# Two attention stages of one encoder layer change places, and their filler products are dealt out anew

## The chip, the cores and the metric

The kernel runs on one core of one Trainium2 chip, in one launch. The metric is the device time of a run in microseconds (us); it was 2349.54 us, the median of three runs (2349.14 to 2350.11). All arrays are fp32. Products on TensorE (PE) are made accurate by splitting each operand into a rounded high part and a low rest and doing three passes (low by high, high by high, high by low). The other engines are VectorE (DVE), ScalarE (ACT), GpSimd (POOL); SyncE (SP) issues nearly all DMAs.

## The reference, cut to what matters

One layer is computed for two request groups with shared weights: a prompt of 1024 positions, and a sample of 64 new positions that follow 2048 cached ones.

```python
h    = rms_norm(x, g_pre_mix)
u_a, v_a, q, k, v_b = split(h @ w_in)                      # 5 blocks of 1024 columns
y_a  = gelu(u_a) * (tril(w_s[g]) @ layer_norm(gelu(v_a)) + b_s)
# stick-breaking attention: 16 heads of 64, strictly causal, no softmax
z    = q @ k.T / 8;  A = sigmoid(z) * prod over later keys of sigmoid(-z);  y_b = A @ v
g_a, g_b = split(sigmoid(h @ w_gate + b_gate))             # 2 x 1024 columns
m    = g_a * (y_a @ w_branch_a) + g_b * (y_b @ w_branch_b)
x    = x + rms_norm(m @ w_o, g_post_mix)
x    = x + rms_norm(conv_ffn(rms_norm(x, g_pre_ffn)), g_post_ffn)
```

For the sample group, `k` and `v_b` are appended to the cache (`cache_sb_k`, `cache_sb_v`), so its attention runs over 2112 keys. The gates need only `h`, branch A only `y_a` and its half of the gates: neither depends on an attention.

## The kernel before, in words

Prompt and sample positions lie side by side in one axis of 1092 columns (2 gap columns, 1024, 2 more, 64), cut into three chunks of 364. A *fill* is one matmul of 128 x 128 weights by one chunk; 24 fills (8 tiles of the inner dimension by 3 passes) make a *group*, and 3 groups a *block* of 128 output columns (72 fills). `feature_part` (line 246) issues them. The weights of a block pass through `Weights` (line 109): SP loads 512 KB into one of two raw buffers, POOL splits them into a high and a low slot (`split_one`, lines 145 to 151), PE waits in `ready`. Two such slots rotate in both attention stages.

The stages run one after the other. Each is an `nc.Block` with an instruction stream of its own for every engine, written out by hand: each engine works through its stream in order, with waits on semaphores. At the end of a stage (`Sems.give_back`, line 86) all engines meet in a barrier, after SP has waited for the last stores.

1. `phase_project`: `h` is made and turned (`hT`, high and low, region r0); 40 blocks of `h @ w_in`; q, k, v, y_a go to DRAM scratch. PE ends with nine transposes (line 467) and POOL with a last low part, then SP stores v.
2. `phase_prompt_attention` (line 668): 16 heads of 4 *windows*; a window is a couple of 128-query tiles (0-1, 2-3, 4-5, 6-7, in the order `TURNS`). The windows are cut into 96 *units*. In a unit PE transposes weights (`turn`), scores the window two further on (`score`, `LEAD` = 2), multiplies fills between the scores, and adds up the unit before (`weighted_sum`). ACT makes two sigmoids of each score (lines 942, 943) and the high parts (952), DVE the running product (`scan`, 990) and the low parts (998), POOL the product of both (`weigh`, 818). The fills are all 16 gate blocks, 1152 of them, 10 to 16 in a unit (`DENSE`), 72 in a head; ACT puts the sigmoid on each group and SP stores it.
3. `phase_sample_attention` (line 1019): 8 pairs of heads in *steps* t = -1 to 8. In step t PE follows `PLAN`: scores z0 to z4 of pair t, transposes A0 to A4 of pair t-1's weights, transposes K0 to K3 of pair t+1's cached keys, and at the end `weighted_sum` of pair t-1. DVE's order in a step is A2, `scan_high`, A3, a gated product, A4, `scan_low`, `weigh_low`, K0 to K3; POOL does `split_v`, `weigh_high`, `split_w`. The transposes go through three PSUM buffers, so item n waits for the low part of item n-3. The fills are the 8 blocks of branch A (576), 72 in each of the steps 1 to 8 (`PIECES`). They need `yaT`, which takes the place of `hT`: in steps -1 and 0 there are no fills, and y_a is loaded in 8 pieces of 546 KB through two stage buffers (`load_ya`), rounded by ACT (`ya_hi`, line 1322) and completed by DVE (`ya_lo`, 1374). DVE multiplies each group by its gate (`gated`, 1380), loaded from scratch, and the product `ta` is stored.
4. `phase_merge`: loads `yb`, multiplies branch B, adds `ta`. Then `phase_output` and `phase_ffn`.

## Time and profile before

| | value |
|---|---|
| median of three runs | 2349.54 us (2349.14 to 2350.11) |
| the profiled execution's own time | 2349.76 us |
| its span (first to last instruction) | 2347.8 us |
| mean granted clock of TensorE | 0.963 of full |
| busy: PE, PE weight load, DVE, ACT, POOL | 92%, 88%, 56%, 32%, 37% of the span |
| project stage, last PE instruction | ends at about 559.5 us |
| prompt attention, PE | 579.5 to 1007.8 us |
| sample attention, PE | 1017.9 to 1252.0 us |
| merge, first matmul | 1273.6 us |

The busy time of an engine is the sum of its instructions' spans; a matmul's span includes its way through the array, so that at full clock fills start every 0.17 us though each is shown with 0.33 us. A PE busy time equal to the length of a stretch means that PE had no gap, not that its array was full. The granted clock is a share of the full one: 1.00 and 0.50 are the two levels (2.4 and 1.2 GHz).

### The profile page before, as it was taken

How to read it: one execution, taken by the hardware profiler on the slowest of the kernel's cores; microseconds unless marked ns; L12 is line 12 of the kernel's file. 1: busy time of each engine (PE TensorE's matmuls, PEld its weight loads, DVE VectorE, ACT ScalarE, POOL GpSimd, SP SyncE). 2: the span in 40 equal slices, each digit the busy share in tenths (PEclk: the TensorE clock that was granted, in tenths of full speed). 3: DMA queues.
4: the chain of work that ended last, by engine and by line, in shares of the span. 5: the costliest groups of instructions: out<-in, count | busy, mean ns of one | idle time of the engine just before them, and what ended most of it. 6: DMA issues, size and time to landing. Idle time of an engine off the chain costs nothing. (4 is left out here: it accounts for less than half of the span.)

```text
span 2347.8 us, 33626 instructions
## 1 busy us (share of the span) xinstructions
PE 2164.0 (92%) x12884; PEld 2056.0 (88%) x12884; DVE 1307.8 (56%) x1719; ACT 747.9 (32%) x1428; POOL 860.8 (37%) x485
## 2 busy tenths in 40 slices
PE   6999999996999999937996989899999999999993
PEld 5999999995999999936996978699999999999992
DVE  5044120000777787745563547666767667677666
ACT  3222102232677777633432122221121211212122
POOL 2335324442555455422543310324243242332404
PEclk9999999998999999978997999899999999999996
DMA  5123224556545554345645442211111111111104
GB/s 168 46 82 138 92 75 150 170 151 171 136 124 140 135 137 120 78 143 161 175 135 183 123 152 94 81 45 46 36 54 36 45 49 32 54 44 36 45 0 162
DMA packets 289092, 237.39 MB, mean 101 GB/s; under 512 B 50950, under 2 KB 265430, under 8 KB 288982
## 3 DMA queue, kind: packets, MB, share of 16 engines
q1 hardware_dynamic: 280240, 222.24, 32.7%
q10 hardware_dynamic: 7510, 9.19, 1.2%
q0 software_dynamic: 1232, 4.46, 0.5%
q8 instruction: 74, 1.21, 0.2%
q14 instruction: 36, 0.29, 0.0%
HBM read 168.51 MB, written 67.33 MB: 100 GB/s over the span
## 5 line engine op out<-in xcount | busy, mean ns | idle before, releaser
L148 POOL TENSOR_SCALAR p_w_hi<-p_w_raw 128x1024 fp32r<-128x1024 f32 x136 | 168.5, 1239 | 897.8 <-PE p_psD L170 418.3
L990 DVE TENSOR_TENSOR_SCAN p_rest<-p_rest 128x896 f32<-128x896 f32 (+7 forms) x128 | 215.4, 1693 | 305.4 <-ACT p_rest L942 305.4
L151 POOL TENSOR_TENSOR p_w_lo<-p_w_raw,p_w_hi 128x1024 fp32r<-128x1024 f32 x136 | 358.7, 2638 | 11.3
L168 PE MATMUL p_psU<-mergedT_lo,p_w_hi 128*128 128x364 f32 x1056 | 347.0, 329 | 2.7 <-ACTq L1878 2.7
L170 PE MATMUL p_psU<-mergedT_hi,p_w_lo 128*128 128x364 f32 x1056 | 347.8, 329 | 0.0
L169 PE MATMUL p_psU<-mergedT_hi,p_w_hi 128*128 128x364 f32 x1056 | 347.5, 329 | 0.0
L257 PE MATMUL p_psB<-hT_lo,p_w_hi 128*128 128x364 f32 x960 | 319.0, 332 | 2.4 <-issue 2.4
L257 PE MATMUL p_psB<-hT_hi,p_w_lo 128*128 128x364 f32 x960 | 316.6, 330 | 0.0
L257 PE MATMUL p_psB<-hT_hi,p_w_hi 128*128 128x364 f32 x960 | 316.0, 329 | 0.0
L1901 DVE TENSOR_TENSOR p_acc<-p_psD,p_acc 128x512 f32<-128x512 f32 (+1 forms) x396 | 273.4, 691 | 46.3 <-PE p_psD L170 45.1
L818 POOL TENSOR_TENSOR p_weights<-p_weights,p_rest 128x895 f32<-128x895 f32 (+7 forms) x128 | 160.2, 1256 | 198.5 <-DVE p_rest L990 198.5
L168 PEld LDWEIGHTS p_psU<-mergedT_lo,p_w_hi 128*128 128x128 f32 x1056 | 199.3, 189 | 5.0 <-POOLq L132 2.9
L169 PEld LDWEIGHTS p_psU<-mergedT_hi,p_w_hi 128*128 128x128 f32 x1056 | 199.1, 189 | 0.8
L170 PEld LDWEIGHTS p_psU<-mergedT_hi,p_w_lo 128*128 128x128 f32 x1056 | 199.2, 189 | 0.0
L257 PEld LDWEIGHTS p_psB<-hT_lo,p_w_hi 128*128 128x128 f32 x960 | 181.4, 189 | 3.4 <-issue 2.8
L531 ACT ACTIVATE p_line<-p_psB 128x364 f32<-128x364 f32 x117 | 55.6, 475 | 403.2 <-PE p_psB L257 403.2
L257 PEld LDWEIGHTS p_psB<-hT_hi,p_w_hi 128*128 128x128 f32 x960 | 181.4, 189 | 0.0
L257 PEld LDWEIGHTS p_psB<-hT_hi,p_w_lo 128*128 128x128 f32 x960 | 181.2, 189 | 0.0
L168 PE MATMUL p_psD<-p_w_lo,p_hid_hi 128*128 128x512 f32 (+1 forms) x396 | 156.4, 395 | 9.4 <-issue 9.4
L169 PE MATMUL p_psD<-p_w_hi,p_hid_hi 128*128 128x512 f32 (+1 forms) x396 | 157.1, 397 | 0.0
L170 PE MATMUL p_psD<-p_w_hi,p_hid_lo 128*128 128x512 f32 (+1 forms) x396 | 156.3, 395 | 0.0
L1874 ACT ACTIVATE p_conv_gate<-p_conv_gate 128x1090 f32<-128x1090 f32 x22 | 24.6, 1116 | 367.6 <-DVE p_conv_gate L1912 367.6
(207 smaller groups left out, 4367.0 us busy)
## 6 DMA issues: line engine op xcount, KB each, us to landing
p_w_raw<-in_w_up SPq DMA_DIRECT2D x44, 512.0 KB, 3.7
p_w_raw<-in_w_in SPq DMA_DIRECT2D x40, 512.0 KB, 3.9
p_w_raw<-in_w_down SPq DMA_DIRECT2D x22, 512.0 KB, 3.5
p_kT_hi<-k_hi_scratch SPq DMA_DIRECT2D x32, 256.0 KB, 4.5
p_kT_lo<-k_lo_scratch SPq DMA_DIRECT2D x32, 256.0 KB, 5.0
p_w_raw<-in_w_gate SPq DMA_DIRECT2D x16, 512.0 KB, 4.0
p_raw_k<-in_cache_sb_k SPq DMA_DIRECT2D x8, 1024.0 KB, 7.7
p_raw_v<-in_cache_sb_v SPq DMA_DIRECT2D x8, 1024.0 KB, 6.2
```

The costliest lines, as they stand in the source:

```text
L148: self.nc.gpsimd.tensor_scalar(self.hi[:, slot, :], self.raw[:, parity, :], 1.0, 0.0, ALU.mult, ALU.add).then_inc(self.split, 1)
L151: self.nc.gpsimd.tensor_tensor(self.lo[:, slot, :], self.raw[:, parity, :], self.hi[:, slot, :].bitcast(F32), ALU.subtract).then_inc(self. ...
L168: nc.tensor.matmul(out, stat_hi, mov_lo, start=first, stop=False)
L169: nc.tensor.matmul(out, stat_hi, mov_hi, start=False, stop=False)
L170: return nc.tensor.matmul(out, stat_lo, mov_hi, start=False, stop=last)
L257: last = nc.tensor.matmul(out[:, 0:CH], stat[:, slot, w], mov[:, k, c], start=(at == 0), stop=(at == 3 * KT - 1))
L531: nc.scalar.activation(line_of(n)[:, c * CH:(c + 1) * CH], psB[:, q % 3, 0:CH], func).then_inc(s("line"), 1)
L818: nc.gpsimd.tensor_tensor(wt[:, b % 6, 0:n - 1], wt[:, b % 6, 0:n - 1], rest[:, b % 4, 1:n], ALU.mult).then_inc(s("weights"), 1)
L990: nc.vector.tensor_tensor_scan(src, src, src, 1.0, ALU.mult, ALU.bypass).then_inc(s("scanned"), 1)
L1874: nc.scalar.activation(cv[0][:, GAP:COLS], cv[0][:, GAP:COLS], ACT.Gelu_apprx_tanh).then_inc(s("gelu"), 1)
L1901: nc.vector.tensor_tensor(acc[0:r, m, w], psD[0:r, share_bank(b, n), :], acc[0:r, m, w], ALU.add).then_inc(s("added"), 1)
```

## The change

The order of the stages becomes project, sample attention, prompt attention, merge. The 16 gate blocks are divided: blocks 0 to 7 (`GATES_WITH_SAMPLE` = 8) are filled into sample attention, blocks 8 to 15 and then, after a changeover, the 8 blocks of branch A into prompt attention. `y_a` takes the place of `h` in the middle of prompt attention.

```diff
+GATES_WITH_SAMPLE = KT
@@ build_layer
-    phase_project(nc, a, o, d, ident, par, hT, r1, region + f_size)
-    phase_prompt_attention(nc, a, d, ident, par, hT, r1, region + f_size)
-    phase_sample_attention(nc, a, d, ident, yaT, r1, region + f_size)
+    phase_project(nc, a, o, d, ident, par, hT, ring, wide_end, end - wide_end)
+    phase_sample_attention(nc, a, d, ident, par, hT, ring, spare(), narrow_end, end - narrow_end)
+    phase_prompt_attention(nc, a, d, ident, par, hT, yaT, ring, spare(), narrow_end, end - narrow_end)
```

The three stages share one weight ring at a fixed place. Each of the first two already loads and splits the first block of the next stage (`load(n + 4)` up to n + 4 = NB in project; `n + 3 <= GB` and `n + 2 <= GB` in sample attention), and the next stage starts with it ready:

```diff
@@ phase_sample_attention
+    FILLED = ("z0", "z1", "z2", "z3", "z4", "A4", "K0", "K1", "K2", "K3")
+    DENSE = {-1: 60, 0: 64, PAIRS: 60}
...
+        total, x, n = DENSE.get(t, 56), FILLED.index(what), len(FILLED)
+        return total * (x + 1) // n - total * x // n
...
+                ring.start_pool(pool, 1)
...
+                    fill(BEFORE[i], dense(t, what))
```

So there are 60 fills in step -1, 64 in step 0, 56 in each of the steps 1 to 7 and 60 in step 8. Loading, rounding and completing y_a, the gate loads and `gated` leave this stage; ACT's `gate` (a sigmoid on each group) and `store_gate` come in. SP issues, in this order: K of pair 0, weights 1, then after `cleared` the new rows of pair 0, K of pair 1, weights 2, V of pair 0. PE begins with fills as soon as `cleared` is signalled, before the first transpose.

```diff
@@ phase_prompt_attention
-    DENSE = {3: (12, 12), 0: (16,), 2: (11, 11), 1: (10,)}
+    SHARE = {3: (12, 12), 0: (16,), 2: (11, 11), 1: (10,)}
+    FIRST, BETWEEN = 60, 48
+    SWAP = range(48, 55)
...
+    COUNTS = (shared_out(9 * KT * GB - FIRST - BETWEEN, range(SWAP.start)) + [0] * len(SWAP)
+              + shared_out(9 * KT * KT, range(SWAP.stop, len(UNITS))))
...
+                            if e == NE:
+                                pe.wait_ge(s("yaT_lo0"), KT // 2)
+                                pe.wait_ge(s("yaT_lo1"), KT // 2)
...
+                fill(0, FIRST)
                 pe.wait_ge(s("mask_made"), 3)
-                for b in range(2 * LEAD):
-                    for part in range(len(parts(tile_of(b)))):
-                        score(b, part)
+                for x, (b, part) in enumerate(pieces):
+                    score(b, part)
+                    fill(cuts[x], cuts[x + 1] - cuts[x])
```

PE starts with 60 fills, then does the six first scores with 8 fills behind each, then units 0 to 47 with 468 fills in the old proportions, units 48 to 54 with none, and units 55 to 95 with 576 fills of branch A. In the changeover the pieces of y_a come one in a unit (two in unit 48): SP loads piece j once piece j-2 is complete, ACT rounds it at the end of its part of the unit, and the low part is made by POOL for the even pieces and by DVE for the odd ones, again at the end of the unit:

```diff
+                def load_ya(j):
+                    if j >= 2:
+                        sp.wait_ge(s(f"yaT_lo{j % 2}"), j // 2)
+                    sp.dma_start(stage[:, j % 2, :], d.ya[j]).then_inc(s(f"ya_ready{j % 2}"), 16)
...
+                def ya_hi(j):
+                    act.wait_ge(s(f"ya_ready{j % 2}"), 16 * (j // 2 + 1))
+                    act.wait_ge(s("group"), NE)
+                    nc.scalar.activation(yaT[0][:, j, :], stage[:, j % 2, :], ACT.Copy).then_inc(s("yaT_hi"), 1)
...
+                    for e in range(max(groups_ended(k), NE), groups_ended(k + 1)):
+                        gated(e)
...
+                    for j in range(1, KT, 2):
+                        if k == swap_unit(j):
+                            ya_lo(j)
```

Pieces 0 and 1 are loaded from unit 44 on. The first four gate chunks are loaded in unit 50, each later one when three older products have been stored. On POOL a unit's weight split now comes ahead of its `weigh`s, and the split of block 1 ahead of the first `weigh`.

## Rows read from the trace of the kernel before

**Rows 1.** The page, part 1: busy us and share of the span.

```profile
PE 2164.0 (92%) x12884; PEld 2056.0 (88%) x12884; DVE 1307.8 (56%) x1719; ACT 747.9 (32%) x1428; POOL 860.8 (37%) x485
```

**Rows 2.** Busy time by stretch: length, PE, PEld, DVE, ACT, POOL, clock, DMA share, GB/s.

```profile
559.50:569.40 9.90, 0.39 (x4) 0.12 (x2) 0.00 (x0) 2.28 (x4) 2.61 (x1) 0.73 0.61 169
569.40:579.40 10.00, 0.00 (x0) 0.00 (x0) 0.00 (x0) 1.28 (x1) 1.75 (x5) 0.50 0.91 208
579.40:599.00 19.60, 14.26 (x49) 11.60 (x50) 12.63 (x7) 8.09 (x19) 15.74 (x8) 0.52 1.01 214
599.00:1008.60 409.60, 407.59 (x2834) 398.92 (x2832) 317.50 (x378) 288.87 (x670) 201.21 (x152) 1.00 0.48 120
1008.60:1073.60 65.00, 13.09 (x53) 10.50 (x53) 30.04 (x25) 17.15 (x26) 18.90 (x10) 0.60 0.57 169
1073.60:1252.00 178.40, 178.36 (x1190) 171.47 (x1188) 98.62 (x123) 69.70 (x142) 81.16 (x33) 0.99 0.51 143
1120.20:1143.20 23.00, 23.00 (x156) 22.10 (x155) 13.79 (x17) 9.92 (x20) 12.10 (x5) 1.00 0.62 174
```

**Rows 3.** Timeline of PE: start, length, line, tile; in brackets the idle time before.

```profile
579.46 0.77 PE L862 MATMUL p_psZ<-p_kT_lo,p_qT 128*128 128x512 f32 x1 [19.57 <-DMA p_qT<-q_lo_scratch]
...
590.13 1.11 PE L879 MATMUL p_psT<-ident,p_weights 128*128 128x128 f32 x4 [3.83 <-POOL p_weights L818]
...
1017.93 3.64 PE L1244 MATMUL p_psR<-ident,p_raw_k 128*128 128x128 f32 x16 [10.15 <-DMA p_raw_k<-in_cache_sb_k]
```

**Rows 4.** Timeline of PE: two fills that follow each other at full clock.

```profile
603.27 0.33 PE L257 MATMUL p_psD<-hT_hi,p_w_hi 128*128 128x364 f32 x1
603.44 0.33 PE L257 MATMUL p_psD<-hT_hi,p_w_lo 128*128 128x364 f32 x1
```

**Rows 5.** Timeline of DVE: first and last clear at the start of sample attention.

```profile
1011.77 0.27 DVE L1389 MEMSET p_q_hi<- 128x256 f32 x1 [3.12 <-PEq L88]
...
1012.71 0.39 DVE L1394 CAST p_mask<-p_mask_plain 64x64 fp32r<-64x64 f32 x2 [0.31 <-POOL p_mask_plain L1202]
```

**Rows 6.** Timeline, one step of sample attention: the chain from A2 to K3.

```profile
1126.27 0.60 PE L1244 MATMUL p_psR<-ident,p_weights 128*128 128x128 f32 x4
...
1128.15 2.42 DVE L1358 TENSOR_TENSOR_SCAN p_rest<-p_rest 128x1088 f32<-128x1088 f32 x1
...
1136.08 1.28 DVE L1346 TENSOR_TENSOR p_kT_lo<-p_psR,p_kT_hi 128x512 fp32r<-128x512 f32 x2
...
1137.29 0.60 PE L1244 MATMUL p_psR<-ident,p_raw_k 128*128 128x128 f32 x4
```

**Rows 7.** Busy time by stretch, third microsecond after PE's end at 1252.0.

```profile
1254.00:1255.00 1.00, 0.00 (x0) 0.00 (x0) 0.00 (x0) 0.00 (x0) 0.00 (x0) 0.50 0.00 0
```

**Rows 8.** Groups by line: busy us, mean ns, idle us before.

```profile
L990 DVE TENSOR_TENSOR_SCAN p_rest<-p_rest 128x896 f32<-128x896 f32 (+7 forms) x128 | 215.4, 1693 | 305.4 <-ACT p_rest L942 305.4
L818 POOL TENSOR_TENSOR p_weights<-p_weights,p_rest 128x895 f32<-128x895 f32 (+7 forms) x128 | 160.2, 1256 | 198.5 <-DVE p_rest L990 198.5
L411 POOL TENSOR_TENSOR p_lo<-p_line,p_hi 128x1092 fp32r<-128x1092 f32 x16 | 41.3, 2580 | 26.5 <-ACT p_hi L546 26.5
```

**Rows 9.** Timeline, two roundings of y_a pieces; DMA issues, us to landing.

```profile
1024.28 1.11 ACT L1322 ACTIVATE yaT_hi<-p_ya_rows 128x1092 fp32r<-128x1092 f32 x1 [4.63 <-DMA p_ya_rows<-ya_scratch]
...
1035.74 1.11 ACT L1322 ACTIVATE yaT_hi<-p_ya_rows 128x1092 fp32r<-128x1092 f32 x1 [8.37 <-DMA p_ya_rows<-ya_scratch]
...
p_ya_rows<-ya_scratch SPq DMA_DIRECT2D x8, 546.0 KB, 5.0
```

**Rows 10.** Timeline of DVE and POOL where their instructions lie beside each other.

```profile
1047.08 2.11 POOL L1195 TENSOR_TENSOR p_weights<-p_weights,p_rest 128x1087 f32<-128x1087 f32 x1 [9.05 <-DVE p_rest L1358]
1047.11 4.23 DVE L1365 TENSOR_TENSOR_SCAN p_rest<-p_rest 128x1025 f32<-128x1025 f32 x1
...
1054.63 5.00 DVE L1374 TENSOR_TENSOR yaT_lo<-p_ya_rows,yaT_hi 128x1092 fp32r<-128x1092 f32 x1
...
1060.15 1.28 DVE L1374 TENSOR_TENSOR yaT_lo<-p_ya_rows,yaT_hi 128x1092 fp32r<-128x1092 f32 x1
```

More of the change, by code:

```diff
@@ L297, in phase_project @@
         f = Place(nc, start, size)
-        ring = Weights(nc, s, Weights.buffers("p1", SLOTS, f, f))
+        ring = Weights(nc, s, weights)
         x_at = f.at
@@ L673, in phase_prompt_attention @@
+def phase_prompt_attention(nc, a, d, ident, par, hT, yaT, weights, small, start, size):
     QT = SEQ // P
@@ L723, in phase_prompt_attention @@
         f = Place(nc, start, size)
-        ring = Weights(nc, s, Weights.buffers("p4", 2, f, f))
+        ring = Weights(nc, s, weights)
         kT_hi = f("p4_kT_hi", [P, 2, SEQ], F32R)
@@ L976, in _ @@
                         sigmoids(b)
-                    for e in range(groups_ended(k), groups_ended(k + 1)):
+                    for e in range(groups_ended(k), min(groups_ended(k + 1), NE)):
                         gate(e)
@@ L980, in _ @@
                         y_low_rows(w - 1)
+                    for j in range(KT):
+                        if k == swap_unit(j):
+                            ya_hi(j)
                 y_low_rows(PW - 1)
```

832 lines of the change are left out of this document (443 added, 389 removed).

## The prediction

> **What bounds the kernel now.** I read the page first: PE is busy 92% of the span, and of the others none over 56% [rows 1]. So time is lost only where PE stands still or runs at half clock. The table of stretches shows where: between PE's last project work at 559.5 us and the end of sample attention at 1252.0 us lie two full stretches, 409.6 us (407.6 busy, clock 1.00) and 178.4 us (all busy, clock 0.99), and three poor ones: 19.9 us almost empty, 19.6 us at clock 0.52, and 65.0 us with 13.1 us of PE work at 0.60 [rows 2]. The timeline names the waits: q from DRAM at 579.46, the first weights at 590.13, K of the cache at 1017.93 [rows 3]; behind it there are no fills until y_a is complete at 1073.6. Where there are fills, PE is full; the loss is where there are none.
>
> **The account of before.** The change touches only the 692.5 us from 559.5 to 1252.0; the merge's idle time behind it stays. At full clock this work takes 409.6 + 178.4 us, less 1.8 us for the clock of 0.99 in the second, plus half of the PE busy time of the two slow stretches (14.3 / 2 + 13.1 / 2 = 13.7 us): 600 us. 92.5 us are lost. The number of fills is the same after (576 + 1152), as are scores, transposes and sums, so the sum for after is 600 us plus its own losses.
>
> **Units.** A fill costs 0.166 us at full clock (start to start, 0.17 in the rows, 0.166 over 24 of them) [rows 4] and about twice that at half. The long prompt stretch holds all but 12 of the 1152 fills, 189 us, so 220.6 us are other PE work: 2.30 us a unit, 13.8 us a head of six units; with 72 fills a head takes 25.7 us. A sample step takes 23.0 us [rows 2], 11.9 us of it fills.
>
> **The losses after, in order.**
>
> *(a) Project to sample: 11.8 us.* The barrier and the stores stay: PE got nothing before 569.4 us [rows 2]. Then PE waits for `cleared`; in the sample stage of before masks and clears took from 1011.8 to 1013.1 us, 1.3 us [rows 5], and I add 0.6 us for the signal. Nothing from DRAM is waited for, since gate block 0 is split already. The extra block in project adds one 512 KB load and one POOL split, about 4 us, two blocks before the end, where POOL idles; if that cover were gone, its last low part would come 4 us later.
>
> *(b) Slow start: 3 us.* The clock is at half after the gap. In the stretch from 1073.6 us, which starts the same way, its mean of 0.99 stands for 1.8 us lost (0.9 to 2.7 with the rounding); in the one from 579.4 us, with sparser work, it was at 0.52 for almost all of 19.6 us [rows 2]. Dense fills are the nearer case; I take 3 us (1 to 5).
>
> *(c) Sample attention: 6 us.* The fills of step -1 stand ahead of K0 (36 of them, 6 us and more) and cover K's arrival; the SP queue also has weights 1 and the new rows in time. What is new is that the filler is thinner. From the transposes A2 (1126.27) to K3 (1137.29) PE takes 11.0 us with 44 fills; with 34 it takes 9.3 us. K3 must wait for the low part of K0, which DVE has ready at about 1136.7, behind two scans, 10.4 us after A2, or 9.9 us without the gated product [rows 6]. That is a new wait of 0.7 us in seven steps, 5 us, plus about 1 us where z0 of step 0 waits for K3's low part. Ends: 0 if the scans meet less POOL work, 12 us if the wait is twice as long. A gate on ACT is not on this chain: ACT is busy 9.9 of 23.0 us. V's load comes later in the step than before (behind A4), with `weighted_sum` some 20 us away; SP's gate stores ahead of it wait only for groups already made.
>
> *(d) Sample to prompt: 3.8 us, and (e) 3 us.* Between PE's end at 1008.6 us and the next stage's first clear lay 3.2 us [rows 2, 5]; with the signal, 3.8 us. PE then has 60 fills, 10 us or more, which cover the 10.0 us that q and k took from 569.4 to 579.46 [rows 2, 3]. In the third microsecond after PE's end at 1252.0 the clock was at half [rows 7], so a second slow start is counted; it may be spared (0 to 3 us).
>
> *(f) First `turn`: 3 us.* Before, the first weights came 10.7 us after the first score began, with 3.83 us of waiting [rows 3]. Now 48 fills (8 us) and six scores (3 us) lie between, which covers the first half of the `turn`; the second half waits for the next POOL product, a mean 1.3 us [rows 8] and its scan, 1.7 us: 3 us (0 to 6).
>
> *(g) The changeover, units 48 to 54: 24 us.* This is the dear part, and no row shows it. PE has 7 x 2.30 = 16 us of work. The pieces of y_a form a loop: rounding 1.1 us, low part on POOL 2.6 us (same shape) [rows 8], issue 0.6 us, landing 5.0 us [rows 9]: 9.3 us for two pieces. ACT's stream stands behind each missing piece, and with it the sigmoids of the next unit, DVE's scans, POOL's products and PE's scores. From the first rounding (3 us into unit 48) to piece 6 it is three loops, 28 us; piece 7 with its low part adds 7 us: 38 us. A second count gives the same. DVE and POOL take turns: the scan of 1025 elements took 4.23 us started beside a POOL product of 2.11 us, and the low part of y_a 5.00 us beside POOL's split of V, 1.28 us alone [rows 10]. So the times add: scans 4608 elements a head at 2.2 ns (2.42 us for 1088, [rows 6]) x 7/6 = 12 us, POOL's products 160.2 / 16 x 7/6 = 12 us [rows 8], low parts 4 x 2.6 + 4 x 1.3 = 16 us: 40 us. I take 40, a loss of 24. Lower end: ACT's work alone, 7 x 3.0 - 2 + 8 x 1.1 = 28 us, a loss of 12. Upper end: loops of 11.5 us as before between two roundings [rows 9], 45 us, and PE's transposes at half clock in the chain, 7 us: a loss of 36.
>
> The Trainium skill (SBUF — State Buffer, section "Who interferes with whom") says that "a DVE instruction with two SBUF inputs contends with a GpSimd instruction that reads SBUF", an exclusive lock; the trace agrees (4.23 and 5.00 us above). By this rule alone, giving the even low parts to POOL saves nothing; were it false, ACT's 28 us would be the pace.
>
> *(h) Slow start behind the changeover: 3 us,* as in (b); 0 if the clock holds.
>
> *(i) Thinner filler in units 0 to 47: 4 us.* 468 fills in 8 heads are 58.5 a head: 9.7 + 13.8 = 23.5 us on PE, where DVE is busy 317.5 / 16 = 19.8 us and ACT 18.1 us [rows 2]. But scans (10.1 us) and POOL (12.6 us, less 0.6 us for fewer splits) take turns: 22.1 of 23.5 us. That fits, with little to spare; I take half a microsecond a head. Ends: 0, and 15 us if the durations of the rows, which include the waiting, simply add (13.5 + 12.0 = 25.5 us a head). Units 55 to 95 have 14 fills each and gated products of 0.5 us on DVE; PE needs 27 us a head there and stays the bound. The gate loads add 4.4 MB there to queues busy half the time.
>
> **Sum.** 11.8 + 3 + 6 + 3.8 + 3 + 3 + 24 + 3 + 4 = 61.6 us, against 92.5: a gain of 31 us. The profiled execution itself took 2349.76 us, 2.0 us over its span and 0.2 us over the median of the runs, so both give 2319 us.
>
> **The rivals.**
>
> 1. *The changeover is light.* ACT's 28 us set it, since the lead of two windows feeds PE; (g) costs 12 and (i) nothing. For it: POOL waits for scans 198.5 us, so it has room [rows 8]. Against it: the turns that DVE and POOL take [rows 10], and only two stage buffers. Gain 31 + 12 + 4 = 47: 2303 us.
>
> 2. *Scans and products become the bound of the thin stretch.* (i) costs 15 and (g) 30: gain 14, 2336 us. For it: 22.1 of 23.5 us. Against it: the rows' durations hold waits that need not remain. If the split of weight block 1 also came late for fill 72 of either stage, so that the early fills did not do what they are for, about as much would be lost.
>
> 3. *The clock falls in the changeover and does not recover; slower.* Place: units 48 to 54 and the thin heads, where PE has gaps. At half clock a thin head needs twice 23.5 us. The gain of 31 us is eaten after 1.3 such heads (8 units); with three, the time is 2319 + 70 = 2389 us. For it: the clock fell soon after work stopped [rows 7]. Against it: it rose in both slow starts with transposes and scores mixed in, and was 1.00 over 409.6 us of the same mix [rows 2]. The Trainium skill (TensorE: Matmul & The Clock Gate, section "HAM oscillation — how this bites in real kernels") describes a kernel whose waits let the clock fall in every round, so that "the HAM transition cost" is paid 32 times instead of once. By that rule the changeover could pay it in each unit; no row here shows gaps of about 1 us at this rhythm.
>
> **How the numbers follow.** Forecast 2319, 0.67; rival 1, 0.15; rival 2, 0.13; rival 3, 0.05. The likeliest case's own range is 2310 to 2329. The range to 8 in 10 takes in rival 1's price and most of rival 2's: 2303 to 2335 us. 0.2% (4.7 us) is about what a measurement of this kernel can tell from none. Faster needs a gain over 4.7 us: all but rival 3 and the far tail of rival 2: 0.92; same 0.03, slower 0.05.
>
> **What would show it.** In the trace after: PE's first fill about 12 us after 559.5; fills through the first two sample steps; K3 transposes waiting under 1 us for K0's low part, in steps of about 21.1 us; PE starting again some 4 us after sample's end; a first `turn` waiting 3 us; one gap-ridden stretch of about 40 us in the middle of prompt attention, with ACT waiting for y_a; heads of 23.5 to 24 us before it and 27 us behind it. Wrong if that stretch is under 30 or over 50 us, if the thin heads take over 25 us, or if the clock is at half anywhere in them.

## The result: 2353.52 us, 0.15% slower, and the profile after

The changed kernel takes 2353.52 us in the median of 20 runs (2348.60 to 2357.63); the kernel before took 2349.57 us in the 20 runs beside it (2348.37 to 2351.69). The ratio is 1.0015, 95% interval 1.0009 to 1.0022: a loss of 4 us, small but clear of the noise. The forecast was 2319 us, with a range of 2303 to 2335 us: the gain of 31 us did not come, and the time lies outside the range.

The page of the kernel after, part 1, answers to [rows 1]. PE holds the same 12884 matmuls and is 14 us longer busy, all of it in the changed stretch; POOL is 46 us longer busy with four more instructions.

```profile
PE 2178.3 (93%) x12884; PEld 2065.2 (88%) x12884; DVE 1315.7 (56%) x1715; ACT 745.7 (32%) x1428; POOL 906.6 (39%) x489
```

The busy time by stretch of the kernel after, with the columns of [rows 2]. In order: project's end to the first fill, sample attention, the gap behind it, prompt attention up to its first `turn`, units 0 to 47, the changeover, units 55 to 95, and what comes behind.

```profile
559.50:571.90 12.40, 1.20 (x9) 0.94 (x9) 1.00 (x5) 3.68 (x5) 3.23 (x4) 0.60 0.52 143
571.90:786.10 214.20, 194.20 (x1240) 183.49 (x1240) 113.85 (x110) 90.09 (x183) 119.32 (x40) 0.96 0.47 128
786.10:789.50 3.40, 0.00 (x0) 0.00 (x0) 0.44 (x2) 0.28 (x1) 0.00 (x0) 1.00 0.04 10
789.50:812.30 22.80, 22.51 (x124) 21.98 (x125) 5.46 (x4) 7.27 (x16) 8.48 (x9) 0.93 1.05 221
812.30:1021.00 208.70, 197.02 (x1352) 189.23 (x1351) 172.37 (x195) 146.94 (x346) 116.58 (x83) 0.98 0.54 136
1021.00:1063.70 42.70, 23.27 (x113) 20.15 (x111) 29.40 (x31) 25.69 (x51) 30.76 (x14) 0.76 0.61 170
1063.70:1256.60 192.90, 190.05 (x1296) 186.19 (x1296) 142.86 (x184) 111.51 (x259) 88.72 (x63) 0.99 0.46 120
1256.60:1278.30 21.70, 0.07 (x2) 0.04 (x1) 3.91 (x7) 3.20 (x3) 4.60 (x3) 0.54 0.83 264
```

Set against the same work at full clock (sample attention 178.4 - 1.8 + 13.1 / 2 = 183.2 us by [rows 2]; units at 2.30 us and fills at 0.166 us), the rows give this ledger:

| step of the prediction | forecast loss | measured loss | how |
|---|---|---|---|
| (a) project to sample | 11.8 | 12.4 | its own row |
| (b), (c) sample attention | 3 + 6 | 31.0 | 214.2 - 183.2 |
| (d) sample to prompt | 3.8 | 3.4 | its own row |
| (e), (f) up to the first `turn` | 3 + 3 | 1.9 | 0.3 idle, 7% of 22.5 for the clock |
| (i) units 0 to 47 | 4 | 20.6 | 208.7 - 48 x 2.30 - 468 x 0.166 |
| (g) changeover | 24 | 26.6 | 42.7 - 7 x 2.30 |
| (h) behind it | 3 | 3.0 | 192.9 - 41 x 2.30 - 576 x 0.166 |
| sum | 61.6 | 98.9 | before: 92.5 |

Two terms failed, and together they are 38.6 us, all of what is missing. The part that I called dear and unseen, the changeover, was right within 3 us. (The full-speed work of the single stages adds up to 1.8 us less than the 600 us of the account. That is why the losses, 98.9 against 92.5, differ by 6.4 us, and the ends of the stretch, 1256.6 against 1252.0, by only 4.6.)

What PE waited for, kernel after, sample attention (column: us in total, times, longest):

```profile
PE p_psR L922 <- DVE p_kT_lo L1024: 16.1, 7, 3.4
PE p_psY L934 <- DMA p_v<-v_lo_scratch: 2.9, 3, 1.2
```

The wait at K3 that the forecast put at 0.7 us in each of seven steps is there seven times, with 2.3 us each in the mean. Of the 31.0 us, 20.0 are idle time of PE (214.2 - 194.2) and 11.0 are busy time above the 183.2 us of work (194.2 - 183.2), and most of this is the clock: it was at 0.50 from 571.9 to 575.7, which is the forecast slow start, and then again in three steps (603.0 to 606.4, 691.8 to 698.6 and 719.1 to 722.5), 13.6 us at half speed, so by my estimate some 7 us lost for which the forecast had no term.

The timeline of the step with the longest wait, on DVE, then POOL, then PE, answers to [rows 6]:

```profile
681.92 3.03 DVE L1036 TENSOR_TENSOR_SCAN p_rest<-p_rest 128x1088 f32<-128x1088 f32 x1
...
685.65 3.64 DVE L1043 TENSOR_TENSOR_SCAN p_rest<-p_rest 128x1025 f32<-128x1025 f32 x1
689.32 2.95 DVE L1047 TENSOR_TENSOR p_weights<-p_weights,p_rest 128x1024 f32<-128x1024 f32 x1
692.19 1.87 DVE L1024 TENSOR_TENSOR p_kT_lo<-p_psR,p_kT_hi 128x512 fp32r<-128x512 f32 x3
...
682.76 4.37 POOL L151 TENSOR_TENSOR w_lo<-w_raw,w_hi 128x1024 fp32r<-128x1024 f32 x1
687.10 4.09 POOL L873 TENSOR_TENSOR p_weights<-p_weights,p_rest 128x1087 f32<-128x1087 f32 x1
...
692.92 1.11 PE L922 MATMUL p_psR<-ident,p_raw_k 128*128 128x128 f32 x4 [3.39 <-DVE p_kT_lo L1024]
```

The same place in the step of [rows 6], kernel before, DVE and then POOL:

```profile
1131.70 3.20 DVE L1365 TENSOR_TENSOR_SCAN p_rest<-p_rest 128x1025 f32<-128x1025 f32 x1
1134.94 1.23 DVE L1369 TENSOR_TENSOR p_weights<-p_weights,p_rest 128x1024 f32<-128x1024 f32 x1
...
1139.29 1.06 POOL L148 TENSOR_SCALAR p_w_hi<-p_w_raw 128x1024 fp32r<-128x1024 f32 x1 [6.53 <-PE p_psD L257]
1140.43 2.41 POOL L151 TENSOR_TENSOR p_w_lo<-p_w_raw,p_w_hi 128x1024 fp32r<-128x1024 f32 x1
```

Read the first of the two from the bottom. PE waits 3.39 us for DVE's low part of K0. DVE comes to it behind two scans and the low weights, and all three are longer than before. POOL splits a weight block (L151) at 682.76, in the middle of DVE's chain, and then does its product of 1087 elements, which took 2.11 us in [rows 10], in 4.09 us. Before, POOL did its split at 1139.29, when DVE's chain was over. (Experiment 1 below shows which of the three owe their length to the split: the scan of 1088 and the low weights. The scan of 1025 is as long without it.)

What PE waited for in units 0 to 47, kernel after:

```profile
PE p_psY L1367 <- DVE p_yb L1498: 5.9, 4, 1.7
PE p_psT L1352 <- POOL p_weights L1282: 5.7, 7, 3.7
```

The timeline of POOL, then DVE, kernel after, with the longest of these waits on PE:

```profile
830.25 1.77 POOL L1282 TENSOR_TENSOR p_weights<-p_weights,p_rest 128x895 f32<-128x895 f32 x1 [2.97 <-DVE p_rest L1483]
832.00 3.02 POOL L148 TENSOR_SCALAR w_hi<-w_raw 128x1024 fp32r<-128x1024 f32 x1
835.10 2.34 POOL L151 TENSOR_TENSOR w_lo<-w_raw,w_hi 128x1024 fp32r<-128x1024 f32 x1
837.41 3.45 POOL L1282 TENSOR_TENSOR p_weights<-p_weights,p_rest 128x1023 f32<-128x1023 f32 x3
...
835.14 4.92 DVE L1483 TENSOR_TENSOR_SCAN p_rest<-p_rest 128x128 f32<-128x128 f32 x2
...
839.57 1.11 PE L1352 MATMUL p_psT<-ident,p_weights 128*128 128x128 f32 x4 [3.67 <-POOL p_weights L1282]
```

The weight split stands at 832.00 between two products of the same head. The second one starts at 837.41, and `turn` waits for it; the scan that it needs had ended at 834.17 (DVE, 831.47 + 2.70), so it comes 3.2 us late. Two short scans of 128 elements on DVE take 4.92 us beside the split. Just behind this wait the clock was at 0.50 for 6.8 us, from 838.6 to 845.4.

### The profile page after: what moved, and what is told of

It reads as the page before. It is cut to its first block and busy times, and to the rows that moved or that the text cites. A ratio compares the mean times of both kernels' runs of the same rounds, so it can differ in the third digit from the quotient of the medians.

```text
span 2352.3 us, 33634 instructions
## 1 busy us (share of the span) xinstructions
PE 2178.3 (93%) x12884; PEld 2065.2 (88%) x12884; DVE 1315.7 (56%) x1715; ACT 745.7 (32%) x1428; POOL 906.6 (39%) x489
## 5 line engine op out<-in xcount | busy, mean ns | idle before, releaser
L271 PE MATMUL p_psB<-hT_lo,w_hi 128*128 128x364 f32 x960 | 319.5, 333 | 2.4 <-issue 2.4
L271 PE MATMUL p_psB<-hT_hi,w_lo 128*128 128x364 f32 x960 | 317.3, 330 | 0.0
L271 PE MATMUL p_psB<-hT_hi,w_hi 128*128 128x364 f32 x960 | 316.6, 330 | 0.0
L148 POOL TENSOR_SCALAR p_w_hi<-p_w_raw 128x1024 fp32r<-128x1024 f32 x72 | 98.3, 1365 | 556.9 <-PE p_psD L170 418.5
L148 POOL TENSOR_SCALAR w_hi<-w_raw 128x1024 fp32r<-128x1024 f32 x64 | 78.0, 1219 | 312.1 <-PE p_psB L271 265.3
L151 POOL TENSOR_TENSOR p_w_lo<-p_w_raw,p_w_hi 128x1024 fp32r<-128x1024 f32 x72 | 191.7, 2663 | 6.0
L271 PEld LDWEIGHTS p_psB<-hT_lo,w_hi 128*128 128x128 f32 x960 | 181.9, 189 | 3.4 <-issue 2.8
L271 PEld LDWEIGHTS p_psB<-hT_hi,w_hi 128*128 128x128 f32 x960 | 181.6, 189 | 0.0
L271 PEld LDWEIGHTS p_psB<-hT_hi,w_lo 128*128 128x128 f32 x960 | 181.5, 189 | 0.0
L151 POOL TENSOR_TENSOR w_lo<-w_raw,w_hi 128x1024 fp32r<-128x1024 f32 x64 | 177.0, 2765 | 5.3
```

The costliest lines, as they stand in the source:

```text
L148: self.nc.gpsimd.tensor_scalar(self.hi[:, slot, :], self.raw[:, parity, :], 1.0, 0.0, ALU.mult, ALU.add).then_inc(self.split, 1)
L151: self.nc.gpsimd.tensor_tensor(self.lo[:, slot, :], self.raw[:, parity, :], self.hi[:, slot, :].bitcast(F32), ALU.subtract).then_inc(self. ...
L271: last = nc.tensor.matmul(out[:, 0:CH], stat[:, slot, w], mov[:, k, c], start=(at == 0), stop=(at == 3 * KT - 1))
```

## The experiments

Two theories for the two failed terms. **Place (S in the sample steps, P in the heads):** each loss is the price of one instruction's place in an in-order stream. Weight splits are now issued wherever a block of fills ends; with 56 fills a step and 58.5 a head this falls elsewhere every time, often ahead of something that PE needs. **Floor (F):** DVE and POOL take turns at SBUF; a head or a step with a split cannot be shorter than about 25.6 and 23 us, and the kernel before stood just on it with its 25.9 and 23.0 us, so that thinner filler can bring nothing.

Heads are measured from one `y_sum` on DVE to the fourth behind it, steps from one masked score to the next. Before, all heads are 25.9 us; after, the thin ones are 30.1, 25.5, 25.7, 22.9, 25.6, 26.0 and 26.0 us, where PE's work alone is 58.5 x 0.166 + 13.8 = 23.5 us. The one of 22.9 us is that of units 20 to 25, the only one in whose units POOL's stream has no weight split (the next, of unit 26, begins at 927.0, near its end at 929.7).

**1. The split of the sample steps at the step's end.**

```diff
-                    for n in range(blocks_ended(i - 1), blocks_ended(i)):
-                        if n + 2 <= GB:
-                            split_w(n + 2)
+                    if what == PLAN[-1] and 0 <= t < PAIRS:
+                        pool.wait_ge(s("weights_low"), t + 1)
+                        for n in range(blocks_ended(i - len(PLAN)), blocks_ended(i)):
+                            if n + 2 <= GB:
+                                split_w(n + 2)
```

> The kernel after, with one edit in sample attention: POOL's weight splits stand at the end of a step and wait for weigh_low of that step, as the group wait placed them in the kernel before. Theory P (the place of the split: it holds the DVE scans up, since DVE and POOL take turns at SBUF): the waits of the K3 transposes shrink from 1.1 to 3.4 us to 0.7 us each, the clock no longer falls in the steps, sample attention shortens from 214 us to 195 to 200 us, the whole from 2353.5 to about 2337 us. Rival T (thinner filler alone: PE reaches the latency chain whatever POOL does): sample attention stays within 4 us of 214, the whole over 2349 us.

Measured: 2342.99 us (2340.77 to 2344.62), ratio to before 0.9969, 0.9957 to 0.9980; sample attention 204.5 us instead of 214.2, between what the two theories gave. The waits of PE in sample attention of this kernel:

```profile
PE p_psY L936 <- DMA p_v<-v_lo_scratch: 8.2, 6, 2.1
PE p_psR L924 <- DVE p_kT_lo L1026: 6.7, 6, 1.2
```

Of 16.1 us at K3, 6.7 are left. The 1088-element scans are back at 2.44 us in the mean (2.77 after) and the low weights at 1.22 (2.34 after); the scans of 1025 elements are not shorter (3.46 and 3.42). With the same instructions in the stretch DVE is busy 11 us less (102.5 for 113.9) and POOL 23 us less (96.5 for 119.3). The clock no longer fell in the steps: it stayed at 1.00 from 574.2 to 779.0. But another wait, hidden before behind the first, comes forward: `weighted_sum` waits for the new values' low part from DRAM. So the place of the split is one cause and not the only one.

**2. The split behind the products of a unit in prompt attention.** POOL's loop over units with `split` written behind the `weigh`s again, as in the kernel before.

> The kernel after, with one edit in prompt attention: a unit's weight split on POOL stands behind its weigh instructions again, as before. Theory P: units 0 to 47 shorten from 208.7 us to 192 to 198 us (the split no longer delays the products that turn waits for), the whole to about 2340 us. Rival T (58 fills a head are too few beside DVE and POOL work that takes turns): units 0 to 47 stay over 204 us, the whole over 2349 us.

Measured: 2352.26 us (2345.26 to 2353.65), ratio 1.0004, 0.9995 to 1.0014: no effect. It was a poor test: "behind the products of unit k" and "ahead of those of unit k+1" are the same place in POOL's stream. Nothing follows for the theories. But it sets one thing right that the description of the change says: the diff writes the split ahead of the `weigh`s, yet by this alone it moves nothing. What moves the split is where the blocks of fills end. Before, with 72 fills a head, each block ended in the last unit of a head; now they end in units 3, 10, 18, 25, 32, 40 and 47.

**3. The changeover in units 42 to 48.** `SWAP = range(42, 49)`.

> The kernel after, with the changeover at units 42 to 48 instead of 48 to 54: 11.1 fills a unit ahead of it instead of 9.75, 12.3 behind it instead of 14.05; all else equal, the split in its new place. Rival T: the waits ahead of the changeover mostly vanish; the 42 units take 42 x 2.30 + 468 x 0.166 = 174 us plus about 4 (at the kernel after's loss of 0.43 us a unit it would be 192), the whole about 2340 us. Theory P: the split still stands in the way, the loss in a unit stays at 0.3 us or more, the whole over 2347 us.

Measured: 2348.62 us (2344.92 to 2353.50), ratio 0.9993, 0.9983 to 1.0002. From the first `turn` to the last fill with h 188.2 us with 42 units; 42 x 2.30 + 468 x 0.166 = 174.3, and about 4 us of these lie behind the last fill, so some 18 us are lost with 11.1 fills a unit, where after it is 20 with 9.75: 0.43 us a unit in both, as theory P had it. Behind the changeover 204.7 us for 203.7 us of work. Denser filler does not take the loss away.

**4. Branch A without y_a.** The branch A products take h; loading, rounding and low parts of y_a are left out, so the branch A output is not that of the layer.

> The kernel after without the loading, rounding and completing of y_a: branch A multiplies hT instead, so its product is another one, and the seven units stay without fills. It prices the changeover's own loop against the lack of filler. If the loop of load, ACT, POOL and DVE sets the 42.7 us: the seven units take 22 to 28 us (scans and products in turn, 24 us by the rows), the whole 15 to 21 us less, 2333 to 2339 us. Rival (the unfilled units are slow by themselves, at half clock): 36 us or more, the whole over 2346 us.

Measured: 2330.10 us (2328.85 to 2331.93), 23 us less than after (ratio to before 0.9914, 0.9897 to 0.9930), and 3 us under the expected times. The seven units without filler, 42.7 us after, in this kernel:

```profile
1021.00:1044.00 23.00, 17.79 (x117) 16.19 (x116) 21.75 (x25) 16.69 (x41) 15.08 (x10) 0.93 0.65 165
```

PE is busy 17.8 of 23.0 us there. So 20 us of the changeover are the work on y_a and its waits, and 7 us (23.0 - 16.1) are lost in these units even without it, with DVE busy 21.8 of 23.0 us. The size of step (g) stands.

**5. The new values loaded at the step's start.** Experiment 1, and:

```diff
                         if t >= 2:
                             store_y(t - 2)
+                            load_new_v(t - 1)
...
-                    if what == "K0" and t >= 2:
-                        load_new_v(t - 1)
```

> The change with the split of the sample steps at the step's end (as in the experiment before), and with the load of a step's new values issued at the start of the step, right behind the store of y, instead of behind K0. Theory S (in the sample steps PE waits for whichever of the masked K products and the new values' low part comes last): the 8.2 us of waits for the DMA of the low part of p_v in 6 steps go, those for the K products stay near 6.7 us, the sample stretch falls from 204.5 to about 197 us and the whole to about 2335 us. Rival (DVE and POOL beside each other set a floor of about 23 us for a step, whatever PE waits for): the DMA waits go and the waits for the K products grow by as much; the steps stay at 22.9 to 23.9 us, the stretch at 203 to 205 us and the whole at 2341 to 2345 us.

Measured: 2333.98 us (2332.99 to 2335.69), ratio 0.9932, 0.9915 to 0.9948; sample attention 195.0 us, steps 21.6 to 21.8 us. The waits of PE there:

```profile
PE p_psR L923 <- DVE p_kT_lo L1025: 6.8, 6, 1.3
```

The DMA wait is gone and the other did not grow, which speaks against the floor of 23 us.

**6. One split per head, at the head's old place.** Only POOL's order (and the loads that follow it) in units 0 to 47:

```diff
+    for k in range(len(UNITS)):
+        pending += [n + 2 for n in range(blocks_ended(k) if k else 1, blocks_ended(k + 1)) if n + 2 < DB]
+        now = k % 6 == 5 or k >= SWAP.start - 1
+        SPLITS.append(pending if now else [])
+        pending = [] if now else pending
...
                     for b in scored(k):
                         weigh(b)
+                    for n in SPLITS[k]:
+                        split(n)
```

> The change with POOL's splits of the weights in the first 48 units of the prompt attention done once per head, behind the products of the head's second tile, where the kernel before had them, instead of wherever a block of fills happens to end. Theory P (it is the changing place of the split that makes the thin heads long: the one head without a split took 22.9 us): the heads of the first half fall from 25.5 to 26.0 us to 23.5 to 24.0 us, the stretch by 10 to 15 us, the whole from 2353 to about 2340 us. Rival F (a split costs what it costs, because DVE and POOL take turns; wherever it lies a head with one takes about 25.6 us): heads stay at or above 25.2 us, the whole within 4 us of 2353 us.

Measured: 2341.69 us (2338.28 to 2344.21), ratio 0.9963, 0.9951 to 0.9974; 12 us less than after. The first seven heads take 23.7 to 24.6 us. Units 0 to 47 up to the last fill with h, to hold against 204.5 us after, and what PE waited for:

```profile
812.40:1003.90 191.50, 189.47 (x1320) 182.99 (x1319) 168.37 (x189) 142.77 (x336) 107.68 (x79) 1.00 0.59 147
```

```profile
PE p_psT L1356 <- POOL p_weights L1289: 2.0, 7, 0.4
```

The same instructions on the same engines (within one of the counts of the kernel after in its 204.5 us), in 13 us less. POOL is busy 5 us less (107.7 for 112.8), DVE as long as before (168.4 in both). The place in POOL's stream, at the moment of the timeline shown of the kernel after, and DVE's scans there:

```profile
834.30 1.99 POOL L1289 TENSOR_TENSOR p_weights<-p_weights,p_rest 128x1023 f32<-128x1023 f32 x1 [2.23 <-ACT p_weights L1428]
836.65 1.31 POOL L1289 TENSOR_TENSOR p_weights<-p_weights,p_rest 128x127 f32<-128x127 f32 x2 [0.36 <-DVE p_rest L1487]
837.93 1.05 POOL L148 TENSOR_SCALAR w_hi<-w_raw 128x1024 fp32r<-128x1024 f32 x1
839.06 2.39 POOL L151 TENSOR_TENSOR w_lo<-w_raw,w_hi 128x1024 fp32r<-128x1024 f32 x1
...
835.19 1.97 DVE L1487 TENSOR_TENSOR_SCAN p_rest<-p_rest 128x128 f32<-128x128 f32 x2
839.36 3.44 DVE L1487 TENSOR_TENSOR_SCAN p_rest<-p_rest 128x640 f32<-128x640 f32 x1 [0.70 <-ACT p_rest L1427]
```

The product comes at 834.30 instead of 837.41, the two short scans take 1.97 us instead of 4.92, and the split behind them takes 3.5 us instead of 5.4. The split still meets a scan, the one of 640 elements: begun 0.3 us behind POOL's low part, it takes 3.44 us, where 2.2 ns an element would give 1.4 (an estimate from the 2.42 us for 1088 of [rows 6]). But at this place PE waits at most 0.4 us. The edit also moves the loads of the weights, as they follow the splits; PE did not wait for weights in this stretch in either kernel.

**7. The kernel before with thinner filler.** 4 of 24 fills left out in each group of both attention stages, so gates and branch A are incomplete:

```diff
+        if thin and at % 5 == 3 and at < 20:
+            continue
```

> The kernel before, with 4 of the 24 fills of each group left out in both attention stages (so the gates and the branch A products are incomplete): 60 fills a head or step instead of 72, with every DVE, POOL and ACT instruction and each split at its old place. Each fill left out is worth 0.166 us of PE: 12 a head are 2.0 us. If PE's own work sets the length of a head (as my forecast took it): heads fall from 25.9 to 23.9 us and steps from 23.0 to 21.0 us, 16 heads and 7 steps bring 46 us, the whole comes to about 2303 us. Rival F (DVE and POOL set a floor just under the old length): heads stay at 25 us or more and steps at 22.5 us or more, the whole falls by less than 15 us, to 2335 us or more. Between the two, the fall shared by the number of heads and steps says where the floor lies.

Measured: 2312.98 us (2311.08 to 2313.84), ratio 0.9842, 0.9825 to 0.9858: 37 us of the 46. Heads 24.2 us (25.9 before), steps 21.8 us (23.0 before). The long stretch, 409.6 us in [rows 2], and one step:

```profile
599.00:981.00 382.00, 378.72 (x2642) 367.01 (x2640) 329.61 (x377) 287.41 (x669) 212.10 (x152) 1.00 0.52 129
1092.40:1114.20 21.80, 21.26 (x145) 20.07 (x144) 13.70 (x18) 9.92 (x20) 12.10 (x6) 1.00 0.68 182
```

A fill left out gave back 1.7 / 12 = 0.14 us in the heads and 1.2 / 12 = 0.10 us in the steps, not the full 0.166 us: something else than the fills begins to show, whether DVE and POOL or another is not settled here. But a floor at 25.6 and 23 us there is not. Theory F falls for these sizes; the result lies between what the two theories gave (2303 us, and 2335 or more).

**8. The low parts of K0 ahead of those of the weights.** Experiment 5, and on DVE:

```diff
                     if what == "A4" and present(t, "z"):
                         scan_low(t)
+                    if what == "K0" and present(t, "z"):
                         weigh_low(t)
```

> The same as the kernel with the earlier load of the new values, and on DVE the low parts of the masked K products of a step ahead of the low parts of the weights instead of behind them. Theory S: the waits for the K products (1.1 us in each of 6 steps) go as well, steps fall to about 21 us, the sample stretch to 190 to 193 us and the whole to about 2329 us. Rival (floor of DVE and POOL): steps stay at 23 us because the weights' low parts, now later, are waited for instead; the stretch stays within 3 us of that of the kernel with the earlier load alone.

Measured: 2326.64 us (2325.21 to 2329.92), ratio 0.9900, 0.9884 to 0.9917. Steps 20.4 to 20.5 us, which is PE's own work: 23.0 - 16 x 0.166 = 20.3. Sample attention, 214.2 us after:

```profile
575.00:763.20 188.20, 187.08 (x1240) 178.31 (x1240) 101.61 (x110) 90.15 (x183) 96.63 (x40) 0.99 0.54 145
```

PE idles 1.1 us in this stretch. DVE is busy 12 us and POOL 23 us less than after with the same instructions, and nearly all of this is there since experiment 1: the excess was time in which the two lay beside each other.

**9. Both mends** (experiments 6 and 8 together).

> The change with both mends together: in the sample steps POOL's split at the step's end, the load of the new values at its start, and DVE's low parts of the masked K products ahead of those of the weights; in the first 48 units of the prompt attention POOL's split once per head behind the products of its second tile. Theory P (each loss sits in a wait of its own, set by the place of one instruction, and the two stretches don't touch each other): the gains add up, 2326.6 us less the 11.5 us of the thin heads (203.1 to 191.6 us), so about 2315 us; sample stretch 188 us, thin stretch 192 us, the changeover unchanged at 47 us from the last fill with h to the first with y_a. Rival F (DVE and POOL in turns set a floor): one of the two stretches gives part of its gain back, 2321 us or more.

Measured: 2313.38 us (2311.80 to 2317.28), ratio 0.9849, 0.9836 to 0.9863; sample 188.0 us, units 0 to 47 191.6 us. The gains add (2315 us expected), so these are two separate losses.

**10. Three buffers for the rows of y_a.** On the kernel after, with each load issued two units ahead:

```diff
-        stage = f("p4_ya_rows", [P, 2, COLS])
+        stage = f("p4_ya_rows", [P, 3, COLS])
...
-                    if j >= 2:
-                        sp.wait_ge(s(f"yaT_lo{j % 2}"), j // 2)
+                    if j >= 3:
+                        sp.wait_ge(s(f"yaT_lo{(j - 3) % 2}"), (j - 3) // 2 + 1)
```

> The change with three buffers for the rows of y_a instead of two, and each load from the fourth issued two units ahead of the unit that rounds it. Theory W (the changeover is long because ACT, in order, waits for the rows: 8.5 us and 5.3 us of DMA wait at the head of its queue, with the evictions of the scores behind it, and each load is issued only when POOL's 4 us low part has freed its buffer): the two waits go, and of the 47 us from the last fill with h to the first with y_a 9 to 13 us go; the whole falls from 2353 to 2340 to 2344 us. Rival V (the eight roundings and low parts themselves, 8.8 us on ACT, 6 to 9 on DVE, 14 on POOL beside the scans, set the length): it stays above 43 us, the whole above 2349 us.

Measured: 2348.58 us (2344.97 to 2350.50), ratio 0.9993, 0.9984 to 1.0002: 5 us less than after, half of what was expected. From the last fill with h to the first with y_a 41.0 us instead of 46.8; but the stretch behind it grew from 193.0 to 196.3 us. The two roundings that waited longest for their rows, kernel after, then in the kernel with both mends and three buffers (experiment 11):

```profile
1034.30 1.11 ACT L1455 ACTIVATE yaT_hi<-p_ya_rows 128x1092 fp32r<-128x1092 f32 x1 [8.47 <-DMA p_ya_rows<-ya_scratch]
...
1051.42 1.11 ACT L1455 ACTIVATE yaT_hi<-p_ya_rows 128x1092 fp32r<-128x1092 f32 x1 [4.99 <-DMA p_ya_rows<-ya_scratch]
```

```profile
996.22 1.11 ACT L1461 ACTIVATE yaT_hi<-p_ya_rows 128x1092 fp32r<-128x1092 f32 x1 [3.85 <-DMA p_ya_rows<-ya_scratch]
...
1017.85 1.11 ACT L1461 ACTIVATE yaT_hi<-p_ya_rows 128x1092 fp32r<-128x1092 f32 x1 [2.49 <-DMA p_ya_rows<-ya_scratch]
```

Of 13.5 us of waits for the rows about 6 are left there, and in experiment 10 itself 3.6 us. Both theories hold in part.

**11. Both mends and three buffers.**

> Both mends of the attention stretches together with the three buffers for the rows of y_a. If the three losses are separate: the time of the kernel with both mends (about 2315 us) less what the three buffers bring by themselves (9 to 13 us by theory W, under 4 us by rival V): 2302 to 2306 us, or 2311 to 2315 us. If it comes out over 3 us above its own sum, the stretches share a resource and the ledger of losses is incomplete.

Measured: 2312.55 us (2309.96 to 2313.41), ratio 0.9836, 0.9823 to 0.9850: 1 us less than without the three buffers in the medians, which is not clear of the noise (2311.80 to 2317.28 there). Of the two sums on record it is the one of rival V. The changeover shrank from 45.9 to 42.1 us, and the stretch behind it grew from 192.0 to 195.8 us. The first 6 us with y_a, in the kernel of experiment 9, then in this one:

```profile
1023.60:1029.60 6.00, 6.00 (x40) 5.91 (x41) 3.23 (x5) 2.30 (x6) 2.08 (x2) 1.00 0.42 88
```

```profile
1020.60:1026.60 6.00, 6.00 (x20) 5.80 (x21) 1.79 (x3) 1.74 (x4) 0.00 (x0) 0.50 0.41 87
```

At clock 0.50 PE does 20 matmuls in the time of 40, which costs 3 us here, and the clock fell once more from 1132.5 to 1135.9. The stretch is 3.8 us longer, just what had been won. This can't be put down to the shorter changeover, though. Experiments 5 and 8 differ only in DVE's order in sample attention; their changeovers hold the same edits and take 47.0 and 46.9 us, and yet the clock was 0.54 and 0.72 in the first 6 us with y_a, and the stretches behind take 195.5 and 193.0 us.

**12. All low parts of y_a on DVE,** on top of experiment 11. POOL's loop over the even pieces goes; DVE's runs over all eight.

> The kernel with both mends and three buffers for the rows of y_a, with all eight low parts of y_a on DVE instead of the even four on POOL. Theory T (DVE and POOL take turns at SBUF, so their times add: in the changeover DVE is busy 38.1 and POOL 34.9 of 43.0 us): four POOL instructions of 2.5 to 4.0 us, 12.5 us, become four on DVE of about 1.3 us, 5 us; the 42.1 us from the last fill with h to the first with y_a fall to 34 to 37 us, and the whole from 2312.6 to 2305 to 2308 us. Rival V (ACT's order and the one rounding per unit set the pace, or the clock, which was 0.50 in the 6 us behind the shorter changeover, gives the gain back): the changeover stays above 40 us, or the stretch behind it grows from 195.8 us by what is gained; the whole stays within 3 us of 2312.6 us.

Measured: 2307.03 us (2305.89 to 2308.30), ratio 0.9811, 0.9797 to 0.9824. This is the fastest version, 1.9% under the kernel before and 46 us under the kernel after. From the last fill with h to the first with y_a 39.4 us, where 34 to 37 were expected by one theory and over 40 by the other; behind it 191.5 us instead of 195.8. The changeover in this kernel, and the first 6 us with y_a:

```profile
978.00:1014.00 36.00, 23.86 (x132) 20.65 (x130) 35.39 (x38) 27.60 (x57) 24.02 (x13) 0.81 0.68 192
1015.70:1021.70 6.00, 6.00 (x40) 5.92 (x41) 3.23 (x5) 2.30 (x6) 1.18 (x1) 1.00 0.33 71
```

DVE is busy 35.4 of 36.0 us (its waits beside POOL included), and PE's longest waits are for it: as far as the rows tell, it is now the bound of the changeover. Less than half of the gain is the shorter changeover (2.7 us); the larger part is the clock, which was at 1.00 when the fills began (4.3 us). The edit does not account for that part, and so the hit on the whole time (2305 to 2308 us expected) is in part luck.

The stretches of the kernels side by side, in us (from the first fill to the end of sample attention; then from the first `turn` to the last fill with h, from there to the first with y_a, and from there to the end of prompt attention). Beside the median, each row is one profiled execution:

| kernel | median | sample | units 0 to 47 | changeover | behind |
|---|---|---|---|---|---|
| after | 2353.52 | 214.2 | 204.5 | 46.8 | 193.0 |
| 5: split and load of the sample steps | 2333.98 | 195.0 | 203.1 | 47.0 | 195.5 |
| 8: sample steps mended | 2326.64 | 188.2 | 203.1 | 46.9 | 193.0 |
| 6: heads mended | 2341.69 | 214.2 | 191.6 | 47.1 | 195.5 |
| 10: three buffers alone | 2348.58 | 213.7 | 204.1 | 41.0 | 196.3 |
| 9: both | 2313.38 | 188.0 | 191.6 | 45.9 | 192.0 |
| 11: and three buffers | 2312.55 | 188.2 | 191.6 | 42.1 | 195.8 |
| 12: and DVE alone | 2307.03 | 187.8 | 191.6 | 39.4 | 191.5 |

## Why the prediction was wrong, step by step

**(a), (b), (d): right.** 12.4 us for 11.8, 3.4 for 3.8, and for the slow start the 3.8 us at half clock from 571.9, so about 2 us lost for 3. **(e), (f): 4 us too dear,** 1.9 us for 6: the first `turn` waited for nothing, and the second slow start cost little, since the early fills ran at a clock of 0.93.

**(c): the first failed step.** I priced the new wait at K3 by the chain of [rows 6], "behind two scans, 10.4 us after A2", with the durations that these rows show. They are durations of a step in which POOL split its weights after this chain. The change moves the end of a block of fills, and the split with it, into the chain, where in the step shown DVE's scan of 1088 elements takes 3.03 us instead of 2.42, its low weights 2.95 instead of 1.23, and POOL's product 4.09 instead of 2.11. The wait came out at 2.3 us instead of 0.7 in each step, beyond the end of "twice as long". Behind it stood two more with nearly the same due time, which I did not follow: the load of the new values' low part (I had looked at V's load only), and the order of DVE's low parts. And with such waits in the steps the clock fell in three of them, for which the sum had no term in this stage. Experiments 1, 5 and 8 take the three waits away one by one: 9.7, 9.5 and 6.8 us. What is left, 188.2 - 183.2 = 5.0 us, is 1.1 us of idle time and 3.9 us of busy time above the work (some 2 of them for the 4.0 us at half clock at the start); so with the mends the wait of (c), forecast with 5 us, is all but gone (0.4 us, once).

**(i): the second failed step.** My argument was a sum: 22.1 us of DVE and POOL in turn fit into 23.5 us of PE, so half a microsecond a head is enough. As a bound the sum was sound; experiment 6 has the same instructions, and its thin heads take 24.1 us in the mean, where 23.5 + 0.5 were forecast; PE idles 2.0 of 191.5 us there. What it left out is the order. 58.5 fills a head do not divide into blocks of 72, so the split falls into another unit in each head, at 832.00 right between two products. The nearest that the forecast comes to this is a sentence of rival 2 ("If the split of weight block 1 also came late"), but there PE would have waited for the weights, and for one block only; here it waits for the products behind the split. Measured 20.6 us, above my upper end of 15: 11.7 us of idle time (2.0 left in experiment 6), some 3.4 us for the 6.8 us at half clock, and about 5.5 us that are neither. These last are there in experiment 6 too (its loss is 20.6 - 13.0 = 7.6 us by the measure of the ledger), and their cause stays open.

**(g): right in size, in part by luck.** 42.7 us for 40, a loss of 26.6 for 24. Both counts behind it had a part in it: the waits of the loop (experiment 10 takes 5.8 us of the length; from the first rounding to that of piece 6 it is 33.7 us, where three loops gave 28) and the turns of DVE and POOL (experiment 12). Without y_a 7 us of the loss stay (experiment 4). But the 26.6 us are 19.4 us of idle time and 7.2 us of busy time above the work, at a mean clock of 0.76, and the clock stood only in my upper end, not in the 24.

**(h): right** at 3.0 us, but not as forecast: PE is idle for 2.9 of them, and waits 1.8 us for a product and 1.0 us for a sum of DVE. The clock was at half for 3.4 us only, and the unit price of the ledger is about 1 us too high here.

Of the signs of being wrong that the forecast named, two came: the thin heads took over 25 us, and the clock was at half in one of them.

**The rivals.** Rival 1 fell (the changeover was not light). Rival 2 named one of the two right places, (i), and its 2336 us are nearest among the likelier cases, but for a cause that the runs refute: scans and products are not the bound of the thin stretch, since the same ones fit into 191.6 us. Rival 3 fell in size: the clock did fall in the thin heads and in the changeover (at 0.50 for 6.8 of 208.7 us and for 20.5 of 42.7 us), but it came back each time. The forecast had no case in which two places of the split, one in each stage, fail together, and this is what the 5% for slower missed. With both mended the kernel takes 2313.38 us, 6 us under the 2319 us of the forecast; that the two lie so close is no proof of the other terms, since the mends also take away the wait that (c) had priced.

The Trainium skill (SBUF — State Buffer, section "Who interferes with whom") names the lock between a DVE instruction with two SBUF inputs and a GpSimd instruction that reads SBUF. The trace agrees again: 2.95 for 1.23 us (DVE's low weights) and 4.37 for 2.41 us (POOL's low part) where the two lie beside each other. I had used the rule for the sum of a head and for the changeover, and not for where in a step the two would meet.

**Still open.** In the first 6 us with y_a the clock was 1.00 in experiments 9 and 12, 0.72 in the kernel after, 0.54 in experiment 6 and 0.50 in experiments 10 and 11. Why was not settled, nor whether it is the same in each execution of a kernel, as each was profiled once; it is worth up to 4 us. What keeps a fill left out from giving back its full price in experiment 7 (0.03 to 0.07 us are missing) was not taken apart, nor were the 5.5 us of step (i).

## What to carry to other kernels

When filler is thinned or moved, list everything that is issued by its progress (splits, loads, stores) and find for each the new place in its engine's stream: a count of busy time per period says whether it can fit, and only the order says whether it does. Behind a wait on a chain with little slack look for the next two with nearly the same due time, since each comes forward when the one before it is mended. Tie preparatory work to a place in the consumer's period, behind the product that PE needs next, and not to the moment at which a block of filler ends. And before a few microseconds behind a stretch of gaps are put down to an edit, look at the clock's row there.

## What the runs showed of the hardware

- A DVE scan of 128x1088 took 2.42 us alone and 3.03 us beside POOL's weight split; POOL's low part of 128x1024 took 2.41 us alone (before, 1140.43) and 4.37 us beside two scans; DVE's product of 128x1024 1.23 and 2.95 us. In experiment 6 the order is the other way round: POOL's low part, begun first, kept its 2.39 us, and the scan of 640 elements begun 0.3 us later took 3.44 us.
- The busy times of a profile hold such waits. Moving one POOL instruction a step out of DVE's chain took 11 us of busy time from DVE and 23 us from POOL in sample attention (experiment 1), with no instruction less.
- The level of the clock when dense fills begin behind a stretch of gaps differed between kernels whose edits lie far from it: 0.54 and 0.72 in the first 6 us in experiments 5 and 8, and 195.5 and 193.0 us for the same work. From experiment 9 to 11 the changeover fell by 3.8 us, its mean clock was 0.74 and 0.83, and yet the fills behind it began at 1.00 in the one and at 0.50 in the other.
